# The first mixture-of-experts gather split in two: two experts ahead of the first expert, two inside the second expert's gate-up

## The reference

```python
def moe_ffn(h, router_w, router_b, w_gate_up, b_gate_up, w_down, b_down):
    ...
    logits = ht.astype(jnp.float32) @ router_w.astype(jnp.float32) + router_b.astype(jnp.float32)
    top_vals, top_idx = lax.top_k(logits, TOP_K)
    weights = jax.nn.softmax(top_vals, axis=-1)
    combine = jnp.sum(jax.nn.one_hot(top_idx, N_EXPERTS, dtype=jnp.float32) * weights[..., None], axis=1)
    ...
    for e in range(N_EXPERTS):
        gu = ht @ w_gate_up[e] + b_gate_up[e]
        gate, up = gu[:, :D_FF], gu[:, D_FF:]
        gate = jnp.minimum(gate, SWIGLU_LIMIT)
        up = jnp.clip(up, -SWIGLU_LIMIT, SWIGLU_LIMIT)
        act = gate * jax.nn.sigmoid(SWIGLU_ALPHA * gate) * (up + 1.0)
        out = out + combine[:, e:e + 1] * (act @ w_down[e] + b_down[e])
```

## Time and profile before

| | us |
|---|---|
| median of 3 runs | 1285.59 (1283.9 to 1288.06) |
| the profiled execution, its own time | 1283.8 |
| its span in the profile | 1282.0 |
| PE busy | 1186.3 (93%) |
| DVE busy | 407.2 (32%) |
| ACT busy | 264.6 (21%) |
| HBM read | 454 MB, mean 355 GB/s |

### The profile page before, as it was taken

How to read it: one execution, slowest core, us unless ns; L and a number is a source line. 1 busy time by engine, 2 the same in 40 slices (tenths; PEclk the granted TensorE clock), 3 DMA queues, 4 the chain that set the end, 5 groups by cost and what they waited for, 6 DMA issues and landing times.

```text
span 1282.0 us, 13964 instructions
## 1 busy us (share of the span) xinstructions
PE 1186.3 (93%) x5960; PEld 611.9 (48%) x5960; DVE 407.2 (32%) x687; ACT 264.6 (21%) x398; POOL 0.2 (0%) x4
## 2 busy tenths in 40 slices
PE   7999999999999999999999888988998898889985
PEld 6799968888743343343334324322432343243321
DVE  6578968856621112112122111211111121111111
ACT  6765545344410010010011001000100010010001
POOL 0000000000000000000000000000000000000000
PEclk9999999999999989999999999999899999999999
DMA  9354425588699999999999999999999999999994
GB/s 324 111 155 132 132 66 164 164 301 334 242 369 428 426 411 429 428 426 429 427 428 426 427 429 428 427 427 428 428 428 427 427 427 430 427 427 428 427 428 201
DMA packets 66075, 455.99 MB, mean 356 GB/s; under 512 B 6777, under 2 KB 23450, under 8 KB 39004
## 3 DMA queue, kind: packets, MB, share of 16 engines
q1 hardware_dynamic: 64292, 454.25, 86.9%
q10 hardware_dynamic: 1720, 0.82, 0.2%
HBM read 454.00 MB, written 1.05 MB: 355 GB/s over the span
## 4 chain that ended last, share of the span: by engine, by line
PE 64%; DMA 29%; DVE 4%; ACT 2%; issue 1%; SPq 0%; ACTq 0%; DVEq 0%
DMA ring<-in_w_gate_up 28%; PE bank L1048 20%; PE bank L1064 12%; PE total L766 7%; PE bank L766 5%; PE total L754 4%; PE bank L754 3%; PE bank L805 3%; PE bank L1029 1%; PE bank L1055 1%; PE bank L829 1%; ACT xn_area L1429 1%; PE total L1075 1%; DVE qk_area L1860 1%; DVE qk_area L1855 1%
## 5 line engine op out<-in xcount | busy, mean ns | idle before, releaser
L1048 PE MATMUL bank<-ring,hy_area 128*64 128x512 f32 x2048 | 456.0, 596 | 38.4 <-DMA ring<-in_w_gate_up 38.4
L1048 PEld LDWEIGHTS bank<-ring,hy_area 128*64 128x64 f32 x2048 | 140.4, 137 | 326.7 <-issue 249.9
L1064 PE MATMUL bank<-ring,xn_area 128*64 128x512 f32 x1024 | 233.4, 609 | 21.6 <-ACT xn_area L1429 21.6
L1852 DVE TENSOR_SCALAR qk_area<-bank 128x512 f32<-128x512 f32 x32 | 22.1, 692 | 424.6 <-PE bank L1048 424.6
L1064 PEld LDWEIGHTS bank<-ring,xn_area 128*64 128x64 f32 x1024 | 72.2, 140 | 161.3 <-issue 133.0
L1865 DVE SCALAR_TENSOR_TENSOR xn_area_r<-bank,tmp_area,xn_area_r 128x512 fp32r<-128x512 f32 x32 | 24.0, 751 | 309.9 <-ACT xn_area_r L1434 309.9
L1425 ACT ACTIVATE qk_area<-qk_area 128x512 f32<-128x512 f32 x32 | 20.2, 631 | 494.5 <-DVE qk_area L1852 494.5
L1544 DVE TENSOR_TENSOR front_r<-ring,slot_r 128x1024 fp32r<-128x1024 f32 x66 | 80.0, 1222 | 38.3 <-ACT slot_r L1263 38.2
L1263 ACT CAST slot_r<-ring 128x1024 fp32r<-128x1024 f32 x66 | 68.9, 1047 | 63.5 <-PE bank L766 28.0
L1434 ACT ACTIVATE xn_area_r<-bank,tmp_area 128x512 fp32r<-128x512 f32 x32 | 22.0, 687 | 236.6 <-PE bank L1064 236.6
L829 PE MATMUL bank<-tmp_area_r 128*128 128x512 f32 x128 | 39.5, 431 | 7.1 <-DVE qk_area L1853 5.3
(11 more groups left out here) (344 smaller groups left out, 1198.5 us busy)
## 6 DMA issues: line engine op xcount, KB each, us to landing
ring<-in_w_gate_up SPq DMA_DIRECT2D x116, 2048.0 KB, 30.4
ring<-in_w_down SPq DMA_DIRECT2D x58, 2048.0 KB, 33.7
ring<-in_w_in SPq DMA_DIRECT2D x31, 1024.0 KB, 5.6
ring<-in_w_gate_up SPq DMA_DIRECT2D x24, 1024.0 KB, 9.1
ring<-in_w_down SPq DMA_DIRECT2D x12, 1024.0 KB, 8.6
ring<-in_w_branch_gla SPq DMA_DIRECT2D x4, 1024.0 KB, 5.0
ring<-in_w_branch_hy SPq DMA_DIRECT2D x4, 1024.0 KB, 8.4
ring<-in_w_out SPq DMA_DIRECT2D x4, 1024.0 KB, 7.1
```

The lines of the kernel that those rows point to most:

```text
L1048: last = pe.matmul(banks[bk][half * CAP:(half + 1) * CAP, :], xeT[:, j, q, :], slot(where(j))[:, c:c + 512], start=False, stop=(j == GU_CH ...
L1064: last = pe.matmul(banks[2][half * CAP:(half + 1) * CAP, :], half_of(actT, f), slot(where(j))[:, c * D + half * 512:c * D + (half + 1) * 512],
```

## The change

Experts 0 to 3 no longer share one gather of 256 columns. Fills for experts 0 and 1 (128 columns each) are done where the whole gather was; fills for experts 2 and 3 (another four of 128 columns) go between chunks 4 to 7 of expert 1's gate-up. `slot_weights(0)` moves from behind expert 0's gate-up to behind its down product, where `spread_rows(0)` stood, and `spread_rows(0)` goes behind chunk 0 of expert 1. On DVE `take_weights` for group 0 leaves `swiglu` and comes after it, and the selection matrix of group 1 is built during expert 2 and not expert 0. The counts of the semaphores follow. What concerns only the skipped loop at the end is left out here.

```diff
--- before.py
+++ after.py
@@ -606,6 +606,10 @@
             return moe_loaded[s], count
 
+        def gathers(e):
+
+            return (e // 2 if e < QUAD else e // QUAD + 1)
+
         def d_cols(d):
 
@@ -794,15 +798,16 @@
                 pe.matmul(begin(name)[:, :], dft[:, a, ri * P:(ri + 1) * P], src, start=True, stop=True).then_inc(fill(name), 1)
 
-            def gather_fill(k, bank_of, width):
-
-                per = 512 // width
+            def gather_fill(k, bank_of, experts):
+
+                per = 2 if experts else DB
                 for i in range(per):
                     d = k * per + i
+                    at = i * 512 // per
                     for m, src in enumerate(hn_parts):
                         for a in range(TB):
-                            moving = sel4[:, a, :, 0:CAP] if width > CAP else more_sel_r[:, a, 0:CAP]
-                            last = pe.matmul(banks[bank_of][:, i * width:(i + 1) * width], src[:, a, d_cols(d)], moving,
+                            moving = sel4[:, a, experts[0]:experts[-1] + 1, 0:CAP] if experts else more_sel_r[:, a, 0:CAP]
+                            last = pe.matmul(banks[bank_of][:, at:at + max(1, len(experts)) * CAP], src[:, a, d_cols(d)], moving,
                                              start=(m == 0 and a == 0), stop=(m == 1 and a == TB - 1))
                 last.then_inc(xe_psum, 1)
@@ -811,7 +816,7 @@
                     for b in range(TB) if d else (a,):
                         for m, src in enumerate(hn_parts):
-                            last = pe.matmul(banks[3][:, d * SEQ:(d + 1) * SEQ], src[:, b, d_cols(d)], sel4[:, b, :, 0:CAP],
+                            last = pe.matmul(banks[3][:, d * SEQ:d * SEQ + 2 * CAP], src[:, b, d_cols(d)], sel4[:, b, 0:2, 0:CAP],
                                              start=(b == 0 and m == 0), stop=(b == 1 and m == 1))
@@ -1086,16 +1091,16 @@
             pe.wait_ge(sel_ready, 1)
             gather_first(1).then_inc(xe_psum, 1)
-            gather_fill(1, 2, QUAD * CAP)
+            gather_fill(1, 2, range(2))
 
             def rest_of_first_gather(j):
 
                 if j == 0:
                     pe.wait_ge(xeT_act, 1)
-                    gather_fill(2, 3, QUAD * CAP)
+                    gather_fill(2, 3, range(2))
                 elif j == 1:
                     pe.wait_ge(xeT_dve, 1)
-                    gather_fill(3, 2, QUAD * CAP)
+                    gather_fill(3, 2, range(2))
                 elif j == 4:
                     pe.wait_ge(comb_ready, 1)
@@ -1107,11 +1112,23 @@
             def start_scatters(j):
 
-                if j == 1:
+                if j == 0:
+                    pe.wait_ge(cslot_ready, 1)
+                    spread_rows(0)
+                elif j == 2:
                     pe.wait_ge(selT_ready, 1)
                     spread_rows(1)
-                elif j in (2, 3):
-                    start_total(j)
+                elif j in (1, 3):
+                    start_total(2 + j // 2)
+                elif j >= 4:
+                    k = j - 4
+                    if k == 0:
+                        pe.wait_ge(selT_ready, 2)
+                    elif k == 1:
+                        pe.wait_ge(y_ready, 1)
+                    else:
+                        pe.wait_ge([xeT_act, xeT_dve][k % 2], 3)
+                    gather_fill(k, 3 - k % 2, range(2, QUAD))
 
             for e in range(E):
                 g, q = e // QUAD, e % QUAD
@@ -1121,13 +1138,11 @@
                 def arrived(j):
                     pe.wait_ge(*moe_arrival(e * CH + j))
-                    if j < GU_CH and j % 2 == 0 and q == 0:
-                        pe.wait_ge([xeT_act, xeT_dve][j // 2 % 2], 2 * g + 1 + j // 4)
+                    if j < GU_CH and j % 2 == 0 and (e == 2 or q == 0):
+                        pe.wait_ge([xeT_act, xeT_dve][j // 2 % 2], 2 * gathers(e) + 1 + j // 4)
 
                 if e == 0:
                     gate_up(q, where, arrived, rest_of_first_gather)
-                    pe.wait_ge(xeT_act, 2)
-                    slot_weights(0)
                 else:
                     if e == 1:
                         gate_up(q, where, arrived, start_scatters)
@@ -1146,21 +1161,22 @@
                     for k in range(FILLS):
                         if k == 2:
-                            pe.wait_ge(xeT_act, 2 * g + 3)
+                            pe.wait_ge(xeT_act, 2 * gathers(e + 1) + 1)
                         if k == 3:
-                            pe.wait_ge(xeT_dve, 2 * g + 3)
-                        gather_fill(k, 3 - k % 2, QUAD * CAP)
-                    pe.wait_ge(xeT_act, 2 * g + 4)
+                            pe.wait_ge(xeT_dve, 2 * gathers(e + 1) + 1)
+                        gather_fill(k, 3 - k % 2, range(QUAD))
+                    pe.wait_ge(xeT_act, 2 * gathers(e + 1) + 2)
                     slot_weights(g + 1)
                     pe.wait_ge(cslot_ready, g + 2)
-                    pe.wait_ge(xeT_dve, 2 * g + 4)
+                    pe.wait_ge(xeT_dve, 2 * gathers(e + 1) + 2)
+                if e == 1:
+                    pe.wait_ge(xeT_act, 4)
+                    pe.wait_ge(xeT_dve, 4)
                 if e < E - 1:
                     pe.wait_ge(up_clipped, e + 1)
                     bias(e + 1)
                 if e:
                     pe.wait_ge(selT_ready, e + 1)
-                else:
-                    pe.wait_ge(cslot_ready, 1)
                 pe.wait_ge(act_ready, e + 1)
                 turn_act()
@@ -1169,7 +1185,7 @@
                 down(where, arrived)
                 if e == 0:
-                    spread_rows(0)
+                    slot_weights(0)
                 elif e < E - 1:
                     spread_rows(e + 1)
...
@@ -1410,14 +1426,15 @@
                             sigmoid_tile(n, a, empty(n))
 
-            def scale_fill(k, bank_of, width, count):
-
-                per = 512 // width
+            def scale_fill(k, experts, count):
+
+                per = 2 if len(experts) > 1 else DB
                 sc.wait_ge(xe_psum, count)
                 for i in range(per):
                     d = k * per + i
-                    dst = xeT[:, d, :, :].rearrange("p q s -> p (q s)") if width > CAP else xeT[:, d, 0, :]
-                    last = nc.scalar.mul(dst, banks[bank_of][:, i * width:(i + 1) * width], col(C_N2D + d))
+                    at = i * 512 // per
+                    last = nc.scalar.mul(xeT[:, d, experts[0]:experts[-1] + 1, :].rearrange("p q s -> p (q s)"),
+                                         banks[3][:, at:at + len(experts) * CAP], col(C_N2D + d))
                 last.then_inc(xeT_act, 1)
 
@@ -1437,16 +1454,19 @@
                 nc.scalar.activation(expo[:, a, :], logit[:, a, 0:E], ACT.Exp, bias=m1n[:, a:a + 1]).then_inc(expo_ready, 1)
             for k in (0, 2):
-                scale_fill(k, 3, QUAD * CAP, k + 1)
+                scale_fill(k, range(2), k + 1)
             filled(sc, "turned")
             nc.scalar.copy(posT, bank("turned")[0:E, 0:SEQ]).then_inc(turned_ready, 1)
             nc.scalar.copy(combT, bank("turned")[E:2 * E, 0:SEQ]).then_inc(turned_ready, 1)
             for e in range(E):
                 g = e // QUAD
+                if e == 1:
+                    for k in (0, 2):
+                        scale_fill(k, range(2, QUAD), FILLS + k + 1)
                 sigmoid(e + 1)
                 if e % QUAD == QUAD - 1 and e < E - 1:
                     for k in (0, 2):
-                        scale_fill(k, 3, QUAD * CAP, FILLS * (g + 1) + k + 1)
+                        scale_fill(k, range(QUAD), FILLS * gathers(e + 1) + k + 1)
                 copy_actT(e + 1)
                 weigh_y(e, (e + 1) * CH, g + 1)
...
@@ -1817,12 +1837,13 @@
                     nc.vector.tensor_tensor(hT[:, 4 * n:4 * n + 4, a * P:(a + 1) * P],
                                             bank(t)[:, :].rearrange("p (k t) -> p k t", k=4), w, ALU.mult).then_inc(empty(t), 1)
-            def scale_fill(k, count):
+            def scale_fill(k, experts, count):
 
                 dve.wait_ge(xe_psum, count)
                 for i in range(2):
                     d = 2 * k + i
-                    last = nc.vector.tensor_scalar(xeT[:, d, :, :].rearrange("p q s -> p (q s)"), banks[2][:, i * SEQ:(i + 1) * SEQ],
+                    last = nc.vector.tensor_scalar(xeT[:, d, experts[0]:experts[-1] + 1, :].rearrange("p q s -> p (q s)"),
+                                                   banks[2][:, i * SEQ:i * SEQ + len(experts) * CAP],
                                                    col(C_N2D + d), None, ALU.mult)
@@ -1835,7 +1856,7 @@
             nc.vector.tensor_copy(both[:, :, E:2 * E], comb[:, :, 1:1 + E]).then_inc(comb_ready, 1)
             for k in (1, 3):
-                scale_fill(k, k + 1)
+                scale_fill(k, range(2), k + 1)
             dve.wait_ge(turned_ready, 2)
```

(21 more changed lines are left out.)

## The result

| | before | after |
|---|---|---|
| median, us | 1285.55 (8 runs, 1283.9 to 1288.06) | 1291.21 (8 runs, 1290.17 to 1293.48) |
| ratio of times | | 1.0049, 95% interval 1.0039 to 1.0058 |
| profiled execution, its own time | 1283.8 | 1290.66 |
| span | 1282.0 | 1288.9 |

The change costs 5.7 us by the medians and 6.3 by the ratio (5.0 to 7.5 by its interval). I had said 1297, in a range of 1289 to 1300: slower as forecast, by half of the amount forecast. What came out is the first rival (1290 to 1292), and the "likeliest case alone", 1294 to 1300, did not.

The account below looks back on a forecast made before the run. Bound by the DMA from its last pause, ended by PE. PE terms 3.05 + 1.88 + 8.0 + 0.3 = 13.2 us, taken as 12 at the end: 1283.8 to 1295.8, with 1.8 to the median 1297; range 1289 to 1300.

Parts of the forecast that it names:

- the first rival: Narrow fills cost only their weight load, 120 ns each; PE plus 6.4 us, end at 1290 to 1292; chance 0.32.
- likeliest case alone: The range given for the main forecast by itself, without the rivals: 1294 to 1300 us; chance 0.58.
- What bounds the kernel: The DMA from its last pause on; a late PE ends the pause, with the ring nearly dry at chunks 36 and 60.
- The price of a narrow fill matmul: A fill matmul with 128 columns in the gathers was taken at 230 ns, between 70 and 230, with 118 as floor.
- four passes: Reading of a 128-column fill matmul by the float32 rows: four passes, 215 ns, and 15 ns extra, 230 ns.
- the second rival: The ring's stock absorbs PE's lateness, at 70 ns per narrow matmul; end about 1286.5, no change; chance 0.07.
- The first chunk comes 1.3 us later, not sooner: Expert 0's first chunk, behind the first gather's start, was to come 14 x (0.230 - 0.138) = 1.3 us later.
- Slot weights worth nothing where they stood and 1.88 where they went: Removing them behind expert 0's gate-up saves nothing, as PE waits for DVE anyway; behind its down product they add 1.88 us.
- The tail in expert 1, 0.3: Before expert 1's down product, DVE must scale the last fill before it may clamp: plus 0.3 us.
- Seams: Extra 0.21 us for a fill between gate-up chunks: two counted in the first gather, three in expert 1.
- From PE to the end: Chunk 36 goes out 13.2 us later, at 417.7 us; the end moves by 11 to 13, taken as 12.
- 2.1 us of stock at chunk 36: Transfer still outstanding in the ring when chunk 36 is issued in the kernel before: 0.9 MB, 2.1 us.

Follow-up runs that it names:

- dummy_e9: The kernel before with 32 extra unread fill matmuls of 256 columns behind chunks 4 to 7 of expert 9's gate-up; 1286.08 us, ratio 1.0001 to before.
- slot_moved: The kernel before with only group 0's slot weights moved behind expert 0's down product and the row spreads reordered, gather left whole; 1287.84 us, ratio 1.0014 to before.
- fill64: The changed kernel with 64-column fills in both gathers of group 0, rows of experts 0 and 2 alone; a single execution, 1290.4 us.
- after_single: The changed kernel with chunks 32 to 63 loaded one at a time and not in pairs; 1291.20 us, ratio 1.0043 to before.

## Why the prediction was right, and where it was off

The direction and the place of the loss were right for the reasons given. The size was not: the range held the result because its low end was the first rival's, which had a chance of 0.32 against 0.58 for the forecast.

- **What bounds the kernel: right.** The DMA from its last pause on. Chunk 36 was issued to a dry queue, at 411.4 us where 417.7 was forecast, and dummy_e9 shows that PE work behind that region is free.
- **The price of a narrow fill matmul: wrong, and this is the step that failed.** I took 230 ns; it is 118. The text had the right number as its floor, from the one-column records, and passed over it for a bet on four passes, since the nearest rows "by size of the moving side" were float32. Size of the moving side was the wrong likeness: the rows that load the same weights and stream less were the nearer ones. My 13.2 us on PE were 6.9 (411.39 against 404.48), 6.3 too many: 3.3 in the first gather (7.3 forecast, 0.89 + 0.94 + 1.09 + 1.09 = 4.0 measured) and 3.6 in the second (8.0 against 4.4), less the 0.6 of seams below. The 81 ns of the second rival did not show either: no fill came under 118 ns per matmul, not with 64 columns.
- **"The first chunk comes 1.3 us later, not sooner": wrong with it.** It starts 1.84 us behind the first gather's start, before 1.99.
- **Slot weights worth nothing where they stood and 1.88 where they went: right.** The DVE distance in expert 0 is 2.05 us after as before, and 1.88 us stand between down and gate-up.
- **The tail in expert 1, 0.3: right** (4.82 us from the last fill to the down product, 4.46 before).
- **Seams: short by 0.6.** I gave the seam to the fills alone. A gate-up chunk that runs by itself takes 1.87 us, four in a row 7.02, so each interrupted chunk pays 0.1 too; all eight chunks of expert 1 now stand alone.
- **From PE to the end: right.** The sum had 2.1 us of stock at chunk 36 and 1.3 of restart, 0.8 us of cover in all; the runs show 0.7 to 1.1. Where the clock stays up it let the pause at 464 us, 1.2 us, drop out as well, and where it falls nothing was covered; the runs show 0.6 to 1.3 won back with the clock up, and all of PE's lateness at the end with it down. Both outcomes for expert 3 occurred. (The last step of the sum, 1295.8 + 1.8, is 1297.6 and not 1297.)
- **The second rival's ground, that the stock absorbs it**, was too small by far at 6.9 us; slot_moved, at 2 us, shows the edge of it.
- The clock in the last down product, 1.7 us, is a term the sum did not have. It goes either way from run to run.

## What to carry to other kernels

Price a matmul whose weights change each time by the larger of a measured floor and its stream: where the floor is the larger (here 118 ns; the rows with 1 to 256 moving columns lie between 113 and 135), narrower moving data saves nothing, and doing the work in two narrow halves costs it twice. With a weight ring, find the last pause of the DMA and what PE must reach to end it; PE work ahead of that point is at the end almost in full, and work well behind it was free here. Before reading a gain out of two single profiles, see that the clock did the same in both: a fall in one place moved the landing by 1.8 to 1.9 us. And before betting on an unseen price, put the forecast on the measured floor unless a row contradicts it.

## What the runs showed of the hardware

An fp32r matmul with 128 x 128 weights takes 118 ns with 64 or 128 moving columns (fill64, the change) and 120 with 256 (before); there is no penalty for few columns. The granted clock fell to the 1.2 GHz level behind the 16 one-column records of a group change, or in the last expert, in some executions and not in others of the same kernel, and the 7.09 us down product behind it took 8.7 to 10.0 (8.70 and 9.98 both in dummy_e9). At expert 3, where the ring was nearly dry, the fall moved the last landing by 1.8 to 1.9 us. Of the 2.1 us of transfer outstanding at chunk 36 in before, 0.7 to 1.1 covered a late PE. Transfers of 1 MB in place of 2 MB ran at 421 to 423 GB/s and not 427 to 430 (after_single, the change).
